# Cached sample pages fetched by indirect gathers instead of one transfer per page

## The reference, cut to what matters

```python
lat_past = cache_kv_latent[l][page_table].reshape(DEC_BATCH, n_pages * PAGE_SIZE, KV_LORA)
kr_past = cache_k_rope[l][page_table].reshape(DEC_BATCH, n_pages * PAGE_SIZE, QK_ROPE)
q_lat = jnp.einsum('bthd,chd->bthc', q_nope, w_uk)
s_past = (jnp.einsum('bthc,bkc->bhtk', q_lat, lat_past)
          + jnp.einsum('bthr,bkr->bhtk', q_rope, kr_past)).astype(jnp.float32) * scale
p = jax.nn.softmax(jnp.concatenate([s_past, s_new], axis=-1), axis=-1)
o_lat = (jnp.einsum('bhtk,bkc->bthc', p[..., :P], lat_past)
         + jnp.einsum('bhtk,bkc->bthc', p[..., P:], c_kv))
```

## Time and profile before

| | us |
|---|---|
| median of 3 runs | 2369.8 (2367.28 to 2374.38) |
| the profiled execution, its own time | 2363.25 |
| its span in the profile | 2361.5 |
| page stage in the profile | 211.0 to 322.9 |
| expert stage in the profile | 688.9 to 2361.5 |

### The profile page before, as it was taken

How to read it: one execution, slowest core, us unless ns; L and a number is a source line. 1 busy time by engine, 2 the same in 40 slices (tenths; PEclk the granted TensorE clock), 3 DMA queues, 4 the chain that set the end, 5 groups by cost and what they waited for, 6 DMA issues and landing times.

```text
span 2361.5 us, 22207 instructions
## 1 busy us (share of the span) xinstructions
PE 1403.1 (59%) x6922; PEld 806.3 (34%) x6922; DVE 1196.7 (51%) x2862; ACT 403.7 (17%) x1227; POOL 1110.4 (47%) x1225
## 2 busy tenths in 40 slices
PE   7997787999887578765766333333333333322348
PEld 5875545788775445442433000000000000000012
DVE  2104324511147976468567566576575575674400
ACT  2213223510112121102212101101101101011000
POOL 0004510000024456556666666666666666666662
PEclk9998897999998789886887655555655565565679
DMA  6214633045359899999999999999999999999995
GB/s 200 72 64 130 166 105 125 1 139 158 125 200 329 316 393 377 390 341 380 399 397 371 366 375 363 366 373 375 365 371 369 367 361 375 379 364 369 369 369 189
DMA packets 269164, 687.35 MB, mean 291 GB/s; under 512 B 36039, under 2 KB 119912, under 8 KB 269039
## 3 DMA queue, kind: packets, MB, share of 16 engines
q0 software_dynamic: 161792, 579.94, 65.3%
q1 hardware_dynamic: 107255, 106.00, 14.1%
HBM read 681.84 MB, written 4.18 MB: 290 GB/s over the span
## 4 chain that ended last, share of the span: by engine, by line
PE 28%; POOL 23%; issue 13%; DMA 13%; DVE 9%; another core or an unknown queue 8%; SPq 4%; ACT 1%; DVEq 1%; ACTq 0%; POOLq 0%
POOL arena L638 23%; PE bank L669 20%; DMA arena<-in_peer_u_dram,arena 7%; DVE arena L1867 5%; PE bank L1147 5%; DMA arena<-in_peer_v_dram,arena 3%; PE bank L665 2%; DVEq L1803 1%; SPq L513 1%; SPq L509 1%; SPq L510 1%; DMA arena<-in_x_sample_dram 1%; DMA arena<-in_w_pool_out_dram 1%; DMA arena<-in_w_mla_out_dram 1%
## 5 line engine op out<-in xcount | busy, mean ns | idle before, releaser
L1147 PE MATMUL bank<-arena 128*32 128x512 f32 x2176 | 480.7, 949 | 788.7 <-DMA arena<-in_peer_v_dram,arena 730.8
L1867 DVE CUSTOM_DVE_ANT_0 arena<-arena,bank 128x1024 f32<-128x1024 f32 x544 | 655.2, 1220 | 413.4 <-DMA arena<-in_peer_u_dram,arena 378.5
L638 POOL DMA_INDIRECT arena<-in_peer_u_dram,arena x544 | 518.2, 952 | 617.6 <-DVE arena L1852 391.1
L669 PE MATMUL bank<-arena 128*128 128x256 f32 (+7 forms) x2940 | 712.9, 400 | 94.4 <-DVE arena L1769 26.8
L638 POOL DMA_INDIRECT arena<-in_peer_v_dram,arena x544 | 521.8, 959 | 372.9 <-remote 156.3
L669 PEld LDWEIGHTS bank<-arena 128*128 128x128 f32 (+2 forms) x2940 | 547.2, 195 | 268.4 <-issue 108.3
L1147 PEld LDWEIGHTS bank<-arena 128*32 128x32 f32 x2176 | 98.0, 147 | 1139.3 <-issue 1138.3
L1178 ACT ACTIVATE arena<-bank 128x256 f32<-128x256 f32 (+12 forms) x321 | 124.6, 418 | 435.7 <-PE bank L669 167.0
L665 PE MATMUL bank<-arena 128*128 128x128 f32 (+4 forms) x766 | 121.7, 307 | 58.1 <-DMA arena<-in_cache_k_rope_dram 16.9
L630 POOL DMA_DIRECT2D arena<-in_cache_kv_latent_dram x64 | 34.6, 541 | 229.4 <-issue 229.4
L1178 ACT ACTIVATE arena<-arena 32x8 f32<-32x8 f32 x544 | 115.8, 213 | 128.6 <-issue 57.2
(11 more groups left out here) (142 smaller groups left out, 853.5 us busy)
## 6 DMA issues: line engine op xcount, KB each, us to landing
arena<-in_w_in_dram SPq DMA_DIRECT2D x30, 1024.0 KB, 5.8
arena<-in_w_peer_q_dram SPq DMA_DIRECT2D x16, 1024.0 KB
arena<-in_peer_u_dram,arena POOLq DMA_INDIRECT x544
arena<-in_peer_v_dram,arena POOLq DMA_INDIRECT x544
arena<-in_cache_kv_latent_dram POOLq DMA_DIRECT2D x64, 128.0 KB
arena<-in_cache_kv_latent_dram SPq DMA_DIRECT2D x64, 128.0 KB, 2.1
arena<-in_w_o_dram SPq DMA_DIRECT2D x8, 1024.0 KB
arena<-in_cache_mem_k_dram SPq DMA_DIRECT2D x8, 512.0 KB, 5.1
```

Of the source, the lines that this page charges most:

```text
L638: pool.indirect_dma_start(out=ring[s % RING], out_offset=None, in_=table[0], in_offset=IndirectOffsetOnAxis(ap=ix, axis=0)).then_inc(land[ ...
L669: last = pe.matmul(dst, lhs(k), rhs(k), start=(k == 0), stop=(k == n - 1))
L1147: last = pe.matmul(bank[rows_out, c], zw[:, n % 2, QW // 4 * j + m], ring[at_slot[j] % RING][:, c * 512:(c + 1) * 512], start=(first and m ...
L1867: dve.tensor_tensor_reduce(ring[s % RING], ring[s % RING], h_dot, 1.0, 0.0, ALU.mult, ALU.add, act_a[:, n % 2, k:k + 1]).then_inc(u_free, 1)
```

## The change

SP loads no pages any more, and no page number goes through a register. POOL fetches all of them with indirect gathers. The latent cache is read as rows of 4 KB (four tokens), 32 rows to a page, and one gather fetches 128 such rows, which are the four pages of one sequence and one step: partition 32 k + c gets tokens 4 c to 4 c + 3 of page k. A step has four latent gathers (`pages(s)`, 512 KB each) and four rope gathers (`ropes(s)`, 128 rows of 512 B each). The row numbers (page number times 32 plus chunk c) are computed once by DVE, behind its wait for `ld_gain`, from a page table that the load now spreads over all partitions.

The rope values land as (sequence, token, value) in each partition, and the transposes want (token, sequence, value). ACT brings them into that order in `rop_j`, one copy of 128x512 for each step, between `page_exp(s - 1)` and the copy of u = 2. It waits there for the rope gathers (`ld_rope`). TensorE waits for that copy (`rp_ev`) before u = 8.

The latent buffers stay three, the rope buffers become two. POOL's order is: pages 0 and 1, the wait for the pooling stage, ropes 0 and 1, pages 2, ropes 2, and then for each further step pages(s) behind `pv_mm`, s - 2, and ropes(s) behind the copy of step s - 2. The memory loads of b = 0 still wait for `pv_mm` 6; those of b = 1 now wait with b = 2 and b = 3 for the last scores.

```diff
@@ -32,6 +32,8 @@
 XH, XD = 4, 128
 PAGES, PAGE = 16, 128
 PGRP = 4
+CHUNK = 32
+ROWS = PAGE // CHUNK
 LATW = KL + ROPE
 OFF_U, OFF_CQ, OFF_CKV, OFF_KR, OFF_QX, OFF_G = 0, 512, 896, 1152, 1184, 1696
 EH, NKEY, TOPK = 8, 128, 16
@@ -280,8 +282,11 @@
 
         wukT = at(45.5, [H, KL])
         qlat = at(56, [2, NB, H, TS])
-        lat = [at(115.75 + 18 * i, [4, PGRP, KL]) for i in range(3)]
-        rop = [at(131.75 + 18 * i, [PGRP, P]) for i in range(3)]
+        lat = [at(116.25 + 16 * i, [4, ROWS, KL]) for i in range(3)]
+        rop = at(164.25, [2, 4, P])
+        rop_j = at(187.75, [ROWS, P])
+        pidx = at(19.75, [NB, PAGES // PGRP], U32)
+        ctmp, chunk = at(19.875, [2, 16]), at(18.875, [1])
         latT = at(169.75, [4, 2, 512])
         ropT = at(185.75, [512])
         prob = at(45.5, [2, 512])
@@ -372,7 +377,8 @@
             sem, ("hi_mm", "hi_ev", "uo_mm", "uo_ev", "pool_d", "pool_mm", "pool_ev"))
         ld_pool = sem("ld_pool")
         uk_mm, uk_ev, ql_mm, ql_ev = map(sem, ("uk_mm", "uk_ev", "ql_mm", "ql_ev"))
-        ld_page = [sem(f"ld_page{i}") for i in range(3)]
+        ld_rope = [sem(f"ld_rope{i}") for i in range(2)]
+        page_ids, rp_ev = sem("page_ids"), sem("rp_ev")
         ld_smem = [sem(f"ld_smem{i}") for i in range(4)]
         pt_mm, pt_ev, pt_ed, ps_mm, ps_max, ps_exp, pp_mm, pp_ev, pv_mm, pv_ev, ol_done, po_mm, po_ev = map(
             sem, ("pt_mm", "pt_ev", "pt_ed", "ps_mm", "ps_max", "ps_exp", "pp_mm", "pp_ev",
@@ -395,7 +401,7 @@
         pq_mm, pq_ev, sc_mm, sc_ev = map(sem, ("pq_mm", "pq_ev", "sc_mm", "sc_ev"))
 
         land = [sem(f"land{i}") for i in range(RING)]
-        land0 = [16 * 16 * len(range(i, STEPS, 3)) if i < 3 else 0 for i in range(RING)]
+        land0 = [64 * len(range(i, STEPS, 3)) if i < 3 else 0 for i in range(RING)]
         (tk_gap, tk_exp, id_next, idvf, idv_done, gelu_done, w_done, wv_done, z_done, u_free, v_free, acc_free) = map(
             sem, ("tk_gap", "tk_exp", "id_next", "idvf", "idv_done", "gelu_done", "w_done", "wv_done", "z_done",
                   "u_free", "v_free", "acc_free"))
@@ -464,7 +470,7 @@
             sp.dma_start(pscale[:], pool_scale[0].rearrange("(k p) -> p k", p=P), allow_slow_non_contiguous=True).then_inc(ld_gain, 16)
             sp.dma_start(gkv[:], kv_norm.to_broadcast([P, KL])).then_inc(ld_gain, 16)
             sp.dma_start(gffn[:], ffn_norm.to_broadcast([P, D])).then_inc(ld_gain, 16)
-            sp.dma_start(pagetab[0:1], page_table.rearrange("(a b) n -> a (b n)", a=1)).then_inc(ld_gain, 16)
+            sp.dma_start(pagetab[:], page_table.rearrange("(a b) n -> a (b n)", a=1).to_broadcast([P, P])).then_inc(ld_gain, 16)
             sp.dma_start(hist[0:NB * HIST], state_pool[0].rearrange("b t c -> (b t) c")).then_inc(ld_state, 16)
 
             store(pool_s[0][:, 0:HIST - TS], state_pool[0][:, TS:HIST])
@@ -493,35 +499,10 @@
                 sp.dma_start(pool_s[0, b, HIST - TS:HIST], uout[b * TS:(b + 1) * TS, 0]).then_inc(st_pool, 16)
             sp.dma_start(pool_p[0, 0], uout[0:HIST, 1]).then_inc(st_pool, 16)
 
-            sp.wait_ge(qt_mm, 2 * TILES)
-
-            def load_pages(s):
-
-                i, a, g = s % 3, s // 4, s % 4
-                if s == 2:
-                    sp.wait_ge(pool_mm, 2 * PG)
-                    sp.wait_ge(pool_d, PG)
-                if s >= 3:
-                    sp.wait_ge(pv_mm, s - 2)
-                for j in range(2):
-                    for k in range(PGRP):
-                        n = (4 * a + j) * PAGES + g * PGRP + k
-                        page = sp.value_load(pagetab[0:1, n:n + 1], min_val=0, max_val=cache_lat.shape[1] - 1)
-                        sp.dma_start(lat[i][:, j, k],
-                                     cache_lat[0][DynSlice(page, 1)].rearrange("a p c -> (a p) c")).then_inc(
-                            ld_page[i], 16)
-                        sp.dma_start(rop[i][:, k, ROPE * j:ROPE * (j + 1)],
-                                     cache_kr[0][DynSlice(page, 1)].rearrange("a p c -> (a p) c")).then_inc(
-                            ld_page[i], 16)
-
-            sp.wait_ge(ld_gain, 16 * 13)
-            for s in range(STEPS):
-                load_pages(s)
-
             for b in range(NB):
                 if b == 0:
                     sp.wait_ge(pv_mm, 6)
-                elif b == 2:
+                elif b == 1:
                     sp.wait_ge(ps_mm, STEPS)
                 elif b >= 4:
                     sp.wait_ge(mo_mm, b - 3)
@@ -614,25 +595,36 @@
             pool.memset(uP[:, :, 0:HIST], 0.0).then_inc(zeroed, 1)
             pool.memset(eps[:], EPS).then_inc(zeroed, 1)
 
-            pool.wait_ge(ld_gain, 16 * 13)
+            lat_rows = cache_lat[0].rearrange("n (c r) d -> (n c) (r d)", c=CHUNK)
+            rope_rows = cache_kr[0].rearrange("n (c r) d -> (n c) (r d)", c=CHUNK)
+            pool.wait_ge(page_ids, PGRP)
             pool.wait_ge(qt_mm, 2 * TILES)
-            for s in range(STEPS):
-                i, a, g = s % 3, s // 4, s % 4
-                if s == 2:
-                    pool.wait_ge(pool_mm, 2 * PG)
-                    pool.wait_ge(pool_d, PG)
+
+            def pages(s):
+                for j in range(4):
+                    pool.indirect_dma_start(out=lat[s % 3][:, j].rearrange("p r d -> p (r d)"), out_offset=None, in_=lat_rows,
+                                            in_offset=IndirectOffsetOnAxis(ap=pidx[:, 4 * (s // 4) + j, s % 4:s % 4 + 1],
+                                                                           axis=0)).then_inc(land[s % 3], 16)
+
+            def ropes(s):
+                for j in range(4):
+                    pool.indirect_dma_start(out=rop[:, s % 2, j], out_offset=None, in_=rope_rows,
+                                            in_offset=IndirectOffsetOnAxis(ap=pidx[:, 4 * (s // 4) + j, s % 4:s % 4 + 1],
+                                                                           axis=0)).then_inc(ld_rope[s % 2], 16)
+
+            pages(0)
+            pages(1)
+            pool.wait_ge(pool_mm, 2 * PG)
+            pool.wait_ge(pool_d, PG)
+            ropes(0)
+            ropes(1)
+            pages(2)
+            for s in range(2, STEPS):
                 if s >= 3:
                     pool.wait_ge(pv_mm, s - 2)
-                for j in range(2, 4):
-                    for k in range(PGRP):
-                        n = (4 * a + j) * PAGES + g * PGRP + k
-                        page = pool.value_load(pagetab[0:1, n:n + 1], min_val=0, max_val=cache_kr.shape[1] - 1)
-                        pool.dma_start(lat[i][:, j, k],
-                                       cache_lat[0][DynSlice(page, 1)].rearrange("a p c -> (a p) c")).then_inc(
-                            land[i], 16)
-                        pool.dma_start(rop[i][:, k, ROPE * j:ROPE * (j + 1)],
-                                       cache_kr[0][DynSlice(page, 1)].rearrange("a p c -> (a p) c")).then_inc(
-                            land[i], 16)
+                    pages(s)
+                pool.wait_ge(rp_ev, s - 1)
+                ropes(s)
 
             def gather(s, table, ix):
                 pool.indirect_dma_start(out=ring[s % RING], out_offset=None, in_=table[0],
@@ -804,15 +796,16 @@
 
                 i = s % 3
                 if u0 == 0:
-                    pe.wait_ge(ld_page[i], 16 * 16 * (s // 3 + 1))
-                    pe.wait_ge(land[i], 16 * 16 * (s // 3 + 1))
+                    pe.wait_ge(land[i], 64 * (s // 3 + 1))
                 for u in range(u0, u1):
                     n = 9 * s + u
                     if n >= 4:
                         by, count = turn_waits(n - 4)
                         pe.wait_ge((pt_ev, pt_ed)[by], count)
-                    for k in range(PGRP):
-                        src = lat[i][:, u // 2, k, (u % 2) * P:(u % 2 + 1) * P] if u < 8 else rop[i][:, k]
+                    if u == 8:
+                        pe.wait_ge(rp_ev, s + 1)
+                    for k in range(ROWS):
+                        src = lat[i][:, u // 2, k, (u % 2) * P:(u % 2 + 1) * P] if u < 8 else rop_j[:, k]
                         last = turn(bank[:, n % 4, k * P:(k + 1) * P], src, P)
                     last.then_inc(pt_mm, 1)
 
@@ -1317,6 +1310,10 @@
                 turn_out(s, 0)
                 if s >= 1:
                     page_exp(s - 1)
+                    act.wait_ge(pt_mm, 9 * s)
+                act.wait_ge(ld_rope[s % 2], 64 * (s // 2 + 1))
+                copy(rop_j.rearrange("p r (j d) -> p j r d", j=4),
+                     rop[:, s % 2].rearrange("p j (r d) -> p j r d", r=ROWS)).then_inc(rp_ev, 1)
                 for u in (2, 4, 6, 8):
                     turn_out(s, u)
             page_exp(STEPS - 1)
@@ -1540,6 +1537,15 @@
 
 
             dve.wait_ge(ld_gain, 16 * 13)
+            link(tt(ctmp[:], ident[:, 1, 0:NS].rearrange("p (a b) -> p a b", a=2),
+                    iota16.unsqueeze(1).to_broadcast([P, 2, 16]), ALU.mult))
```

(7 more changed lines are left out.)

2 lines of the change are left out of this document (1 added, 1 removed).

## The result

The changed kernel takes **2387.3 us** (median of 4 runs, 2384.4 to 2389.8) against 2368.5 us for the kernel before on the same chip: a ratio of **1.0066, 95% interval 1.0043 to 1.0088**. It is slower; 2339 was forecast. The profiled execution took 2387.0 us, its span is 2385.2.

A forecast was written before the change was run, and what follows sets the result against it. Issue of small page DMAs was taken to bound the page stage at 14 us a step. First step ending at 223 plus 69.2 put last scores at 292.2, 30.7 earlier; 2369.8 - 30.7 gave 2339 us, range 2330 to 2358.

The forecast's parts named there:

- The page issue: Page stage: issuing small page DMAs on SP and POOL, not bandwidth, sets the pace of 14 us a step.
- TensorE's step: Page stage: with data there and the clock full, TensorE takes 9.6 to 10.4 us a step, 69.2 for steps 1 to 7.
- the whole gain: End of page stage: last scores at 292.2 instead of 322.9 us, 30.7 us less, with everything behind moving forward.
- step 0: First step of the page stage: gets longer as rope gathers follow the pooling gate; taken to end at 223 us.
- ACT's copy: Rope reordering on ACT each step: 0.6 to 1.2 us, taken as hidden; up to 4 us in all if slow.
- The row numbers on DVE: Seven small DVE instructions, at most 0.69 us each, at no cost; up to 4.8 us if their cover were gone.
- The later wait of SP's memory loads: Loads of b = 1 wait for the last scores: 3 MB, 8.7 us, covered by TensorE's other work, at no cost.
- The landing: Page stage: latents land 8.2 us and ropes 13.2 us after pages may start, in time with 1.5 to 4 us left.
- POOL's pace: Page stage: eight gathers 1.25 us apart take 10.0 us a step, about TensorE's own; POOL's gathers end at 278.9 us.
- Data comes late: Page stage: slow rope packets make steps 11.8 us of DMA, last scores at 305.4, gain 17.5, time 2352; chance 0.22.
- The gain goes to a later stage: Behind the page stage: loads at fixed times would absorb the gain; 2363 to 2370 us; chance 0.08.
- POOL's gathers are slow beside DVE: Page stage: shared ports stretch a gather's slot to 2.13 us, 14.8 us later, 2384.6; chance 0.06.

The follow-up runs named there:

- kernel with plain DMAs: Changed kernel, but SP brings each step's latents and ropes by eight plain 128-row DMAs, page table left out (wrong pages); 2332.5 us, 0.985 of the kernel before.
- paused kernel: Changed kernel with one 0.38 us POOL memset behind each gather but the first twelve, gathers 1.60 us apart; 2343.1 us, 0.9931 of the kernel before.
- paused hybrid: Changed kernel, but SP loads two of four samples' latents page by page, and a 0.38 us memset follows each gather; 2334.9 us, 0.9894 of the kernel before.

## Why the prediction was wrong

**The steps that held.** The page issue did set the pace, and taking it away is worth what was said. TensorE's step, forecast at 69.2 us for steps 1 to 7 from the earlier trace rows, is 68.8 where nothing holds it; the whole gain, forecast at 30.7 us, is 37.7 in the kernel with plain DMAs (2370.2 - 2332.5), the rest being step 0, which there ends at 216. No kernel with gathers gets that part: step 0 ends at 221.4 or later in all of them. Gathers of both kinds start 1.25 us apart and take 0.94 to 0.96 us, so the rope rows of 512 B cost POOL what the earlier trace rows say. The ropes and latents land in time: no DMA is among TensorE's waits. ACT's copy takes 0.62 to 0.63 us (0.6 forecast). Step 0 ends at 222.0 (223 forecast), with ACT's one wait for ropes, 4.5 us. The row numbers on DVE cost nothing: pooling ends where it did. The later wait of SP's memory loads costs nothing.

**The step that failed** is "TensorE's step": 9.6 to 10.4 us were read where POOL issued plain DMAs, and carried over to steps in which POOL issues gathers 1.25 us apart. With these in flight the mean is 17.0. The landing, POOL's pace and TensorE's pace were each weighed as if the larger of them would decide. But while the gathers follow each other, TensorE's hand-offs to ACT and DVE stop, so a part of POOL's 10 us and TensorE's 9.8 add up instead of overlapping: that sum is the 16 to 21 us of steps 1 to 6. How long a hold lasts was a term that the prediction didn't have, and so put at nothing; it measured up to 8.9 us. POOL, in turn, waits for values that come late (13.07 us before 240.98), so the next burst begins only when TensorE has caught up. The clock adds to it: the granted clock is 0.71 from 251.7 to 260 us, behind such a stop.

**Data comes late** (0.22) was no part of the loss: the engines are 36% busy. It appears in the paused kernel, and there at 304, close to the 305.4 that the rival named, and in step 7 of the paused hybrid. **The gain goes to a later stage** (0.08): no; the stage between even got 4.4 us shorter. **POOL's gathers are slow beside DVE** (0.06) had the right sign and nearly the size (2384.6), and the wrong mechanism: the slot is 1.25 us, not 2.13, and DVE's operations keep their lengths. The Trainium skill ("SBUF — State Buffer", Who interferes with whom) has a single source of contention between engines, the ports that DVE and GpSimd share, and TensorE shares with nobody. The trace agrees for the ports, as the gathers keep 0.95 us beside DVE; what is held here are signals of work that is done, of which that rule says nothing.

**Could the trace of before have told?** Yes. It has gathers in a row beside TensorE once, where the expert stage begins and TensorE and DVE still choose keys. Fourteen gathers were issued there from 688.86 to 706.09. Kernel before, timelines of TensorE and ACT:

```profile
709.29 5.03 PE L669 MATMUL bank<-arena 128*128 128x256 f32 x11 [7.64 <-ACT arena L1178]
```

```profile
708.77 1.21 ACT L1178 ACTIVATE arena<-bank 128x256 f32<-128x256 f32 x4 [14.16 <-remote]
```

ACT waits 14.16 us for a TensorE that waits 7.64 us for ACT, and TensorE's updates come 0.06 to 0.16 us apart at 708.61 to 708.90, 2.5 us behind the last gather of that row. It was the same picture, with the same word "remote". And it wasn't TensorE alone. DVE chooses keys there in a chain of operations with nothing but a DRAIN between them (`step`, L1802), an instruction that waits until DVE's own work is done. From the tenth gather on these stretch too (timeline of DVE):

```profile
703.01 0.29 DVE L1810 MAX8 arena<-arena 128x8 f32<-128x128 f32 x1 [1.77 <-issue]
705.82 0.29 DVE L1825 CAST arena<-arena 128x64 f32<-128x64 uint32 x1 [2.07 <-issue]
```

In the trace 730 of DVE's 749 DRAINs end within 0.1 us of the operation before. In this row one, behind the third gather, is 0.3 us late; then from 699.9 to 708.6, where TensorE's updates come too, five are 0.2 to 2.0 us late. The same stretch of the expert stage shows late DRAINs in every kernel of this document. The prediction read the gathers' own durations there, and not what the other engines did beside them. Read with that row, the rival that a burst stops TensorE would have had a price, by this estimate: 10 us of burst and 9.8 of work, less some overlap, 16 to 19 us a step, and a time above the kernel before.

## What to carry to other kernels

When work is moved to another engine or another form of DMA, look in the trace for a stretch in which that form already runs beside the engines that matter, and read their waits there, not only its own duration. An idle engine put down to "remote", with its partner idle for it at the same time, means that a signal came late; look at what ran meanwhile. Indirect gathers beside a pipeline of short hand-offs are best few and spaced: here a pause of 0.35 us more between them turned 0.4 to 0.7% of loss into 0.7% of gain, and six spaced gathers with the rest as plain DMAs of SP into 1.1%.

## What was unexpected of the hardware

In the changed kernel TensorE's semaphore updates were held for up to 8.9 us (221.96 to 230.84) while POOL issued indirect gathers 1.25 us apart, and came out 0.06 us apart, 1.7 to 2.9 us behind the last gather; with seven small gathers a step the longest hold is 11.9 us. Beside plain DMAs of POOL or SP, at up to 204 GB/s, TensorE's updates come within 0.05 us. In the page stage ACT's and DVE's updates, where they have a record, come within 0.01 us; but DVE's DRAINs in the expert stage are up to 2.4 us late beside such a row of gathers. So the hold seems not to be TensorE's alone; that it is one effect rests on the same times. The hold eases with the distance of the gathers: last scores at 341 or 336 (1.25 us), 318.5 (1.34), 304 (1.60, where POOL's pace already decides), and with four gathers a step the step is 10.8 at 1.25 and 10.0 at 2.76, against 9.8 without gathers. Neither the rows' size nor the transfers by themselves showed an effect.

Where in the chip the signals are held is open: the runs show when, and not through what. As the ends of matmuls are modelled in the profile, that TensorE had finished rests on the updates' spacing and on the waits of both partners. The record of updates itself has holes where gathers run: in the page stage 22 of 235 updates of TensorE, ACT and DVE are missing in the changed kernel, and none in the kernel before or in those with plain DMAs. Whether the recording of the trace has a part in the hold no run can tell, as every timed run here comes with a trace's span and clock.
